# Grouped-query attention: the products with the values run three key tiles behind the scores, in place of two

## What is computed

```python
def attend(qblk):
    s = jnp.einsum('bkgqd,bksd->bkgqs', qblk, kh)
    p = jax.nn.softmax(s, axis=-1)
    return jnp.einsum('bkgqs,bksd->bkgqd', p, vh)
```

## Time and profile before

| what | value |
|---|---|
| median of 3 runs | 3871.25 us |
| the three runs | 3865.63 to 3874.64 us |
| time of the profiled execution | 3866.22 us |
| span of the profiled execution, first to last instruction | 3864.4 us |
| mean granted TensorE clock over the span | 0.984 of full |
| TensorE busy with matmuls, whole span | 3680.7 us (95%) |
| VectorE, ScalarE, GpSimd busy, whole span | 2261.6, 2033.9, 1240.1 us |
| attention of layer 0, first score product to last product with the values | 1101.7 to 1666.3 us |
| attention of layer 1 | 3032.1 to 3597.5 us |

### The profile page before, as it was taken

The page is one execution under the profiler, slowest core; times in us unless marked ns, Lnnn a source line. Parts: engine busy times, 40 slices in busy tenths (PEclk is TensorE's granted clock), DMA queues, the critical chain, the costliest instruction groups (busy, mean ns, idle before and its releaser), DMA issues. The chain is left out here.

```text
span 3864.4 us, 56958 instructions
## 1 busy us (share of the span) xinstructions
PE 3680.7 (95%) x20128; PEld 3322.4 (86%) x20128; DVE 2261.6 (59%) x4277; ACT 2033.9 (53%) x4141; POOL 1240.1 (32%) x966
## 2 busy tenths in 40 slices
PE   8999999999999999969989999999999999999698
PEld 8999999999977777747789999999999777777477
DVE  5233335626558888857652333346266688888575
ACT  5233334722258878756552333347222588788664
POOL 0000011003237776745400000110032477777454
PEclk9999999999999999989989999999999999999899
DMA  4455455248731111036443444352387311110364
GB/s 152 137 141 154 131 146 195 82 113 224 201 86 33 31 34 35 21 112 196 137 156 123 126 143 130 122 195 85 112 229 197 82 34 31 36 33 21 119 190 142
DMA packets 560476, 450.77 MB, mean 117 GB/s; under 512 B 179040, under 2 KB 518464, under 8 KB 557120
## 3 DMA queue, kind: packets, MB, share of 16 engines
q1 hardware_dynamic: 559904, 446.07, 38.8%
q10 hardware_dynamic: 288, 1.05, 0.1%
HBM read 301.25 MB, written 136.32 MB: 113 GB/s over the span
## 5 line engine op out<-in xcount | busy, mean ns | idle before, releaser
L779 PE MATMUL pj_acc<-h_hi,pj_whi 128*128 128x384 f32 x2976 | 1034.3, 348 | 4.6 <-DVE h_lo L1211 4.6
L779 PE MATMUL pj_acc<-h_hi,pj_wlo 128*128 128x384 f32 x2976 | 998.3, 335 | 0.0
L779 PE MATMUL pj_acc<-h_lo,pj_whi 128*128 128x384 f32 x2976 | 998.1, 335 | 0.0
L1804 POOL TENSOR_TENSOR ga_plo<-ga_prob,ga_phi 128x512 fp32r<-128x512 f32 (+1 forms) x594 | 767.0, 1303 | 431.1 <-ACT ga_prob L1746 412.0
L1826 DVE TENSOR_REDUCE pl_mx<-ga_ps_x 128x1 f32<-128x512 f32 (+1 forms) x760 | 511.7, 680 | 142.5 <-PE ga_ps_x L1687 130.1
L779 PEld LDWEIGHTS pj_acc<-h_hi,pj_whi 128*128 128x128 f32 x2976 | 561.0, 189 | 11.5 <-DVE h_lo L1211 5.1
L1744 ACT ACTIVATE ga_phi<-ga_ps_s 128x512 fp32r<-128x512 f32 (+1 forms) x792 | 469.5, 593 | 187.7 <-PE ga_ps_s L1704 181.6
L779 PEld LDWEIGHTS pj_acc<-h_lo,pj_whi 128*128 128x128 f32 x2976 | 561.2, 189 | 6.7
L779 PEld LDWEIGHTS pj_acc<-h_hi,pj_wlo 128*128 128x128 f32 x2976 | 560.1, 188 | 0.0
L1746 ACT ACTIVATE ga_prob<-ga_ps_s 128x512 f32<-128x512 f32 (+1 forms) x792 | 465.5, 588 | 16.6 <-DVE ga_plo L1804 14.1
L1496 POOL TENSOR_TENSOR rq_sw<-rq_sw,rq_trig 128x384 f32<-128x384 f32 x48 | 52.1, 1086 | 1242.5 <-DMA rq_sw<-pj_ring 1242.5
(11 more groups left out here) (231 smaller groups left out, 6578.8 us busy)
## 6 DMA issues: line engine op xcount, KB each, us to landing
pj_w<-in_w_in SPq DMA_DIRECT2D x62, 512.0 KB, 3.7
dl_kv<-dil_kv SPq DMA_DIRECT2D x108, 256.0 KB, 2.9
ml_qk<-mqk SPq DMA_DIRECT2D x72, 384.0 KB, 3.5
proj<-pj_ring SPq DMA_DIRECT2D x132, 192.0 KB, 2.9
fi_z<-proj SPq DMA_DIRECT2D x36, 640.0 KB
rq_trig<-in_trig SPq DMA_DIRECT2D x48, 384.0 KB, 4.0
gqk<-rq_parts SPq DMA_DIRECT2D x48, 384.0 KB, 3.5
ml_kv<-tokmaj SPq DMA_DIRECT2D x72, 256.0 KB, 4.2
```

Source lines behind the costliest of these rows:

```text
L779: mm = pe.matmul(acc[s % 2][:, 0:CHUNK], wt[u][:, t, :], ht[:, t, tok], start=(t == 0 and i == 0), stop=(t == KT - 1 and i == 2))
L1804: vector.tensor_tensor(p_lo[r][:, 0:w], prob[f % 2][:, 0:w], p_hi[r][:, 0:w].bitcast(F32), ALU.subtract).then_inc(sem, 1)
```

## The change

One constant, `LAG = 3`, takes the place of three fixed numbers. TensorE weighs tile f - 3 in its loop over f, in place of tile f - 2, and weighs the last three tiles behind the loop, in place of two. VectorE's pieces of the division are due one tile later, 3 tiles after an item of the sample has ended in place of 2, and 7 after one of the prompt in place of 6. No instruction is added or removed, no buffer, bank or semaphore changes, and every wait keeps its rule.

```diff
+        LAG = 3
+
...
-                if f >= 2:
-                    weigh(f - 2)
+                if f >= LAG:
+                    weigh(f - LAG)
                 for o in rows_at(f):
                     max_rows(o)
-            weigh(NTILE - 2)
-            weigh(NTILE - 1)
+            for f in range(NTILE - LAG, NTILE):
+                weigh(f)
...
                 for o in range(NI):
-                    since = f - FIRST[o + 1] - (6 if ITEMS[o][2] else 2)
+                    since = f - FIRST[o + 1] - (7 if ITEMS[o][2] else LAG)
                     if 0 <= since < pieces(o):
                         reciprocal(o, since)
                         if since == pieces(o) - 1:
                             output(o)
```

## The result

The changed kernel takes 3873.75 us in the median of 20 runs (3867.20 to 3878.01), the kernel before 3866.80 us in 20 runs on the same chip. The ratio worked out from all these runs is 1.0015, with a 95% interval of 1.0008 to 1.0022: slower by 0.15%, 6 us (the two medians are 7 us apart). I had predicted 3857, faster by 14 us. The median of three runs that I had started from, 3871.25, is 4.4 us above that of the 20 runs; from the latter the same forecast would have been 3852. The profiled execution took 3872.90 us (span 3871.1) against 3866.22 (3864.4), so it carries the difference: 6.7 us.

A forecast was written before the change was run, and what follows sets the result against it. TensorE was taken to set the pace. Per layer 3.8 (VectorE's waits) + 1.1 (GpSimd's waits) + 2.3 (stage end) = 7.2 us; two layers, 14.4, off 3871.2 gave 3857 us, range 3846 to 3869.

The forecast's parts named there:

- the collisions: VectorE and GpSimd low halves excluding each other in SBUF; the sum kept those already there and added no new ones.
- the gain of 2.3 us at the end of the stage: From the scores of tile 376 to the last product with the values: of 2.8 us waits, 0.5 stays.
- Rings and banks: Exponential and low-half buffer waits, and the bank and store behind the later multiplication: cost zero.
- Waits for GpSimd's low half ahead of tile 376: TensorE's value products at tiles 82 and 168 wait less for GpSimd: a gain of 1.1 us a layer.
- Waits for VectorE's low half: In the windows of division, most of this wait returns at the maximum products; 3.8 us a layer is gained.
- L1689 would take over L1718's waits: Maximum products' waits for VectorE's reduction rise from 5.2 us to above 12, as value products' waits fall.
- The step behind that: VectorE's backlog in the windows of division, followed tile by tile with fixed steps, the low half always 0.66 us.
- third rival: Slower: VectorE's low halves right behind the division collide with GpSimd's in eleven windows a layer, 0.9 us each; +13, 3884; chance 0.07.
- Rival 2: Every wait ahead of tile 376 returns in full elsewhere; only the end pays, 4.6 us, giving 3867; chance 0.20.
- Rival 1: All waits of TensorE's value products go and none returns, VectorE recovering by itself; about -25 us, 3846; chance 0.10.
- my signs: Right if L1718's waits fall under 3 us, L1689's rise above 12, undisturbed tiles take 1.36, stages near 557.5.
- a sign I had named against me: Wrong if a stage is no shorter than 562 us, or ScalarE shows new waits for the full exponential.

The follow-up runs named there:

- the last experiment: Against the changed kernel, the multiplication ending a division came three tiles later in eight plain windows a layer; 3866.72 us, ratio 1.0000 to the kernel before.
- the kernel with the reduction first: The changed kernel with VectorE's reduction of a tile's maximum product placed ahead of the previous tile's low half; 3899.08 us, ratio 1.0074 to the kernel before.

## Why the prediction was wrong

The steps that failed are two: the collisions, which I had left as they were, and the gain of 2.3 us at the end of the stage.

- **Rings and banks, zero.** Right. No matmul or exponential shows a new wait of those kinds; undisturbed windows of 16 tiles take 21.9 us before and after (tiles 10 to 26: 21.89 both).
- **Waits for GpSimd's low half ahead of tile 376, 1.1 a layer.** They are gone: no row of L1718 for GpSimd stands among the waits after (3.6 us before). Their time can't be told from the next term's.
- **Waits for VectorE's low half, 3.8 a layer.** Gains came: 4.10 us in the stretches that got shorter, against 3.8 + 1.1. That the two sums are close is in part luck, since 82 to 98 alone gives 1.49. What failed is the sentence "My sum keeps these collisions as they were". The change made new ones, and the stretches with losses give 4.88 back. Two of those (26 to 34 and 280 to 296, 1.88 us) hang on the place of the multiplication, by the last experiment, and go with the collision. Those with two items' pieces are mixed: 230 to 248 (0.95) comes with the division, 98 to 116 (0.95) with both halves of the change, and in both backlog and collision go together; 164 to 182 (0.74) comes with the later weighing. In 182 to 198 (0.32, with the division) the low half of tile 191 takes 1.11 us beside the weights' split, 0.67 before. That L1689 would take over L1718's waits was right, and undersized: 22.5 us in place of about 14.
- **The step behind that.** I followed VectorE's lateness with one price for the low half, 0.66 us, at any time. Its price depends on when it starts: 0.62 to 0.69 while GpSimd pauses, up to 1.79 just behind GpSimd's start, though not at every such place (last section). At places like tile 27 VectorE is 1.5 us late, and that is right where GpSimd begins. My third rival had the mechanism, and was wrong about where and how often: it put it into all eleven windows that had started at 2 above a multiple of 4, at 0.9 us each. Of those only two have it (tiles 27 and 291, 0.92 and 0.96 us a window); the other four long ones (111, 243, 371, 375) are in or behind windows with the prompt's overlap that had started on a multiple of 4. Its chance of 0.07 was small for an effect of which the longest rows already showed the size. These rows weren't two low halves, though, as I had read them: VectorE's 1776 ns is tile 311 beside GpSimd's piece of the weights' split, and GpSimd's 2387 ns is tile 82 beside VectorE's large subtraction.
- **The end of the stage, 2.3 a layer.** Wrong. From the scores of 376 to the end it takes 1668.86 - 1641.17 = 27.69 us, less 0.68 for the order: 27.0, where it took 26.9. Weighing later does help there, by 1.2 us when it comes alone (its end less its 370 to 376: 35.62 - 9.88 = 25.74). But with the division one tile later too that is lost again, and the last low half ahead of the end, tile 375, now starts 0.16 us behind GpSimd's:

```profile
1643.06 0.17 DVE L1832 TENSOR_REDUCE pl_nmax<-pl_mx 128x4 fp32r<-128x16 f32 x1
1643.15 1.68 DVE L1806 TENSOR_TENSOR ga_plo<-ga_prob,ga_phi 128x512 fp32r<-128x512 f32 x1
```

```profile
1642.99 1.29 POOL L1806 TENSOR_TENSOR ga_plo<-ga_prob,ga_phi 128x512 fp32r<-128x512 f32 x1 [3.03 <-ACT ga_prob L1748]
```

  Tiles 370 to 376, of which my sum said nothing, are 1.05 us longer, and the low half of tile 371 takes 1.63 us there. No run takes the collision at 371 or 375 away alone, so how much of this is the collision and how much the backlog ahead of it stays open. (In the kernel that skips the low halves' tiles neither is long, and from the scores of 376 to the end it still takes 28.0 us.) So the end is 1.13 us slower in place of 2.3 faster, the second large miss: 3.4 us a layer. I had worked out the 2.3 as if only the weighing moved; the division's new place wasn't in it.
- **The start of the stage**, which I had not looked at, is 1.76 and 0.93 us longer. Half of it is plain: no product with the values stands yet between the scores of tiles 2 and 3, so L1703 of tile 3 waits for ScalarE.

```profile
1106.32 0.77 PE L1703 MATMUL ga_ps_s<-pl_qhi,pl_kboth 128*128 128x512 f32 x1 [0.22 <-ACT ga_prob L1748]
```

  That is 0.22 + 0.16 = 0.38 us a stage, on the path, and belongs to the change. The rest is the clock (last section).
- **Rivals.** Rival 2 (the middle gives nothing, the end alone pays) comes near to weighing alone: the middle lost 1 us, the end gave 1.2 in place of 2.3. Rival 1 was wrong: VectorE doesn't recover by itself. Of my signs, the undisturbed 1.36 us, L1718's waits under 3 us and L1689's above 12 held. The stages of 568 us were a sign I had named against me, and ScalarE's full exponential waits 22.5 us for low halves of VectorE where it waited 14.1. GpSimd's low halves, by which I would have known the third rival, kept their median (1293 ns): it was VectorE's that got longer.

By layer: predicted -7.2; measured +3.3 in the mean. The difference of 10.5 is 4.9 of new losses in the middle, 3.4 at the end, 1.3 at the start, and 0.8 that the gains in the middle fell short; these make 10.4. Of the 1.3 at the start some 0.8 is likely chance (last section).

Open: what a collision at 111, 243, 371 or 375 costs apart from the backlog around it; why the later weighing brings the loss in 164 to 182; and what decides which engine of a pair is held up.

## What to carry to other kernels

The low half of VectorE, which reads two SBUF operands, had no fixed price beside GpSimd's like work (0.62 to 1.8 us here): write down when GpSimd starts, and put such work into its pauses. Moving a wait to another line gained nothing here as long as the engine waited for was late; look for what makes it late, here pieces of optional work in the very tiles that hold an urgent one. A table that places the optional pieces in the free tiles gave 1%, where one tile more of distance without it cost 0.15%.

## What the runs showed of the hardware

**One of the two is held up, and it hides in a duration.** With VectorE 0.07 to 0.20 us behind, its low half ends 0.54 or 0.55 us after GpSimd's at tiles 27, 371 and 375, and at 207 in the kernel with the reduction first. With VectorE ahead, GpSimd is held up. In the kernel with the reduction first, VectorE, then GpSimd:

```profile
1350.81 0.75 DVE L1806 TENSOR_TENSOR ga_plo<-ga_prob,ga_phi 128x512 fp32r<-128x512 f32 x1
```

```profile
1350.96 1.75 POOL L1806 TENSOR_TENSOR ga_plo<-ga_prob,ga_phi 128x512 fp32r<-128x512 f32 x1
```

VectorE's, 0.15 us ahead, takes 0.75; GpSimd's takes 1.75 in place of 1.29.

But the recorded starts don't tell alone which one it is. At tile 75 of the changed kernel VectorE starts 0.08 us behind GpSimd and isn't held up; GpSimd is:

```profile
1214.92 0.62 DVE L1806 TENSOR_TENSOR ga_plo<-ga_prob,ga_phi 128x512 fp32r<-128x512 f32 x1
```

```profile
1214.84 1.85 POOL L1806 TENSOR_TENSOR ga_plo<-ga_prob,ga_phi 128x512 fp32r<-128x512 f32 x1 [1.43 <-ACT ga_prob L1748]
```

Tiles 171, 239 and 339 are alike, and 119 beside the weights' split (0.08 to 0.28 us behind, 0.62 us). What stands directly ahead on VectorE goes with it: over the twelve traces, where a low half of VectorE starts 0.04 to 0.45 us behind one of GpSimd, VectorE is held up in 74 of 80 cases behind a reduction, and GpSimd in 68 of 76 behind a reciprocal or the multiplication. Why stays open.

**The clock at the start of the stage.** In all 24 stages of the twelve traces TensorE is idle for 3.12 to 3.16 us ahead of the stage's first product, after work at full clock. The granted clock falls to 0.50, the 1.2 GHz level, at some point from 1.2 us ahead of that product to 1.6 us behind it, and is back at 1.00, the 2.4 GHz level, 6.0 to 9.8 us behind it. Two stretches of the changed kernel (columns as in the earlier trace rows):

```profile
1101.00:1110.20 9.20, 7.99 (x17) 5.37 (x18) 6.41 (x10) 7.16 (x11) 3.80 (x3) 0.50 0.88 210
1110.90:1120.90 10.00, 10.00 (x45) 7.92 (x44) 7.71 (x12) 7.17 (x14) 6.37 (x5) 1.00 0.91 218
```

The first four products gain nothing from a later fall, since the next one, of the scores of tile 2, waits for ScalarE: before, it starts 3.07 us behind the first product in both layers, though in layer 1 the first three products still ran at full clock. What counts is how long the lower level lasts behind them. Before, its last matmul was the 10th and the 14th of the two stages, after the 17th in both; each takes 0.43 us from start to start where one at full clock takes 0.23. 7 and 3 more at 0.20 are 1.4 and 0.6 us, which with the wait of 0.38 make up the 1.76 and 0.93 of the start.

The place of this last matmul differs between the layers of one kernel and between two runs of one kernel (the change again: 17th and 15th); with the distance at three it was the 11th to the 18th, at two the 10th to the 18th. The first part, counted as in the table above, takes 17.17 to 18.65 us in the six stages at distance two, 18.04 in the mean, and 17.80 to 19.03 in 16 stages at distance three (without the kernel with the reduction first), 18.60 in the mean. The 0.56 us between the means is 0.38 of the wait and a rest that is inside the scatter. So no run shows that the clock belongs to the change, and some 1.6 us of the profiles' 6.7 are likely chance; the ratio of 20 runs stands on its own.
